# The packed token list of a mixture-of-experts stage gathered in two column parts, 352 and 224, with the first pair's products between them

## What is computed

```python
g_w, g_idx = lax.top_k(softmax(x @ w_router_group + b), 1)        # 1 of 4 groups
e_val, e_idx = lax.top_k(logits of the 8 experts in that group, 2)
combine = one_hot(expert_id, 32) * softmax(e_val) * g_w           # per token
gate = jnp.einsum("nd,edf->nef", x, p["w_gate"][l])
up = jnp.einsum("nd,edf->nef", x, p["w_up"][l])
hid = jax.nn.silu(gate) * up * combine
out = jnp.einsum("nef,efd->nd", hid, p["w_down"][l])
```

## Time and profile before

| what | us |
|---|---|
| median of 3 runs | 2022.97 (2018.91 to 2027.98) |
| the profiled execution | 2020.29 |
| its span, first to last instruction | 2017.7 |
| TensorE matmuls busy | 1750.8 (87%) |
| VectorE / ScalarE / GpSimd busy | 531.8 / 252.1 / 44.9 |
| mean granted TensorE clock | 0.94 |

### The profile page before, as it was taken

The page is one execution under the profiler, slowest core; times in us unless marked ns, Lnnn a source line. Parts: engine busy times, 40 slices in busy tenths (PEclk is TensorE's granted clock), DMA queues, the critical chain, the costliest instruction groups (busy, mean ns, idle before and its releaser), DMA issues.

```text
span 2017.7 us, 21998 instructions
## 1 busy us (share of the span) xinstructions
PE 1750.8 (87%) x8222; PEld 983.2 (49%) x8222; DVE 531.8 (26%) x1225; ACT 252.1 (12%) x456; POOL 44.9 (2%) x95
## 2 busy tenths in 40 slices
PE   3899999965999689999779999996879968899995
PEld 1477745321776234444337776442347743344442
DVE  1211200243212503334413021013521133233334
ACT  1110001110200221111021000101110021111111
POOL 0000000010000000000000000000100000000000
PEclk9999999987999689999989999998989987999998
DMA  9333334489633229999943233337883330898991
GB/s 400 130 118 135 126 125 146 157 358 370 262 125 118 91 112 381 393 407 394 367 191 147 100 150 126 125 126 319 342 351 117 139 149 7 344 377 364 380 371 68
DMA packets 32246, 454.38 MB, mean 225 GB/s; under 512 B 3632, under 2 KB 3632, under 8 KB 4752
## 3 DMA queue, kind: packets, MB, share of 16 engines
q1 hardware_dynamic: 27648, 402.67, 50.7%
q10 hardware_dynamic: 2304, 33.56, 4.1%
q0 software_dynamic: 2192, 16.75, 2.1%
HBM read 413.77 MB, written 39.19 MB: 224 GB/s over the span
## 4 chain that ended last, share of the span: by engine, by line
issue 38%; PE 37%; DMA 20%; DVE 2%; POOL 1%; ACT 0%; DVEq 0%; POOLq 0%; SPq 0%; ACTq 0%
PE ps L513 37%; DMA ring<-stream 16%; DMA state_sample_out<-ring 3%; DMA gfs<-gfin 1%; ACT work L863 0%; POOL rstd L430 0%; DVEq L1030 0%; POOL prm L452 0%; SPq L407 0%; POOLq L429 0%; DVE work L1066 0%; DVE xT L1450 0%; DVE ring L1381 0%; DVE stats L1037 0%; DVE hT L1464 0%
## 5 line engine op out<-in xcount | busy, mean ns | idle before, releaser
L513 PE MATMUL ps<-ring,work 128*64 128x512 f32 x1536 | 357.7, 616 | 47.5 <-DMA ring<-stream 38.4
L513 PE MATMUL ps<-ring,hT 128*32 128x128 f32 (+1 forms) x1920 | 320.6, 383 | 18.9 <-ACT hT L863 18.9
L513 PE MATMUL ps<-hT,ring 128*128 128x288 f32 x1280 | 316.0, 410 | 1.7 <-DVE work L1308 1.7
L513 PEld LDWEIGHTS ps<-hT,ring 128*128 128x128 f32 x1280 | 244.8, 192 | 70.9 <-DVE work L1308 1.9
L863 ACT ACTIVATE work<-ps 128x512 f32<-128x512 f32 (+4 forms) x256 | 118.8, 471 | 1171.3 <-PE ps L513 1170.7
L513 PE MATMUL ps<-work,ring 128*128 128x288 f32 x1024 | 249.6, 406 | 5.3 <-DVE work L1402 3.1
L513 PEld LDWEIGHTS ps<-ring,work 128*64 128x64 f32 x1536 | 118.2, 141 | 269.7 <-issue 251.0
L513 PEld LDWEIGHTS ps<-ring,hT 128*32 128x32 f32 (+1 forms) x1920 | 155.4, 137 | 185.2 <-issue 183.4
L513 PE MATMUL ps<-work 128*128 128x288 f32 (+6 forms) x800 | 225.7, 426 | 14.0 <-DVE work L1066 12.1
L513 PEld LDWEIGHTS ps<-work,ring 128*128 128x128 f32 x1024 | 194.2, 190 | 59.9 <-issue 6.6
L513 PEld LDWEIGHTS ps<-work 128*128 128x128 f32 (+2 forms) x800 | 136.4, 197 | 103.8 <-issue 80.5
(11 more groups left out here) (180 smaller groups left out, 763.2 us busy)
## 6 DMA issues: line engine op xcount, KB each, us to landing
ring<-stream SPq DMA_DIRECT2D x192, 2048.0 KB, 9.8
state_sample_out<-ring ACTq DMA_DIRECT2D x16, 2048.0 KB, 8.8
prm<-params POOLq DMA_DIRECT2D x3, 2640.5 KB, 9.5
state_out<-prm POOLq DMA_DIRECT2D x8, 512.0 KB, 8.9
cst<-consts POOLq DMA_DIRECT2D x1, 1649.5 KB, 13.9
xT<-x_in POOLq DMA_DIRECT2D x1, 1152.0 KB, 20.9
y_out<-hT POOLq DMA_DIRECT2D x1, 1152.0 KB, 4.4
v_out<-work POOLq DMA_DIRECT2D x2, 128.0 KB, 5.0
```

The source lines that it names most:

```text
L513: ins = nc.tensor.matmul(out, lhsT, rhs, start=start, stop=stop, **k)
```

## The change

The 576 places are cut in `HEAD` = 352 = 288 + 64 and `TAIL` = 224 columns. The windows of the first pair cannot reach beyond 352: expert 0 begins at 0 and expert 1 at 288 at most, each 64 wide.

- VectorE builds `psel` for the first 352 columns, raises `sel_ready`, and then builds the other 224 and raises it again.
- TensorE gathers 352 columns into each of g0 to g7, then makes the broadcasts and pair 0's gate/up products. Behind these it gathers the 224 columns, two k in a tile, in four new tiles g0 to g3 of pair 0 (banks 5, 6, 7, 5), and goes on with pair 0's transposes. The tile g8 is gone, and the three broadcast tiles move on by a bank.
- ScalarE copies pair 0's windows right behind the head tiles, ahead of the broadcasts, and into a buffer of its own (`first_xs`, over `yslot`), since `psel` is still needed. Behind the SiLU of pair 0 it evicts the four new tiles, then copies the windows of pairs 1 and 2.
- GpSimd waits with the parameter load for the last of the new tiles.

```diff
@@ -27,6 +27,8 @@
 CAP = 64
 OCAP = 128
 PACK = 2 * TOK
+HEAD = TOK + CAP
+TAIL = PACK - HEAD
 HGW = PACK + OCAP
 PAIRS = NE // 2
 NOVER = (2 * TOK) // (CAP + 1)
@@ -81,7 +83,7 @@
     if kind == "ysum":
         return []
     if kind == "route":
-        return ["lg", "lgt"] + [f"h{j}" for j in range(6)] + ["rk", "cnt", "ob"] + [f"g{k}" for k in range(KT + 1)] + ["bc0", "bc1", "bc2"]
+        return ["lg", "lgt"] + [f"h{j}" for j in range(6)] + ["rk", "cnt", "ob"] + [f"g{k}" for k in range(KT)] + ["bc0", "bc1", "bc2"]
     return ["t"]
 
 
@@ -93,7 +95,8 @@
 TILES["ysample"] = (YBANK, used[YBANK])
 used[YBANK] += 1
 for p in range(PAIRS):
-    for name, b in [("gu", p % 2), ("t", 2), ("y0", 3), ("y1", 4)] + [(f"c{ft}", 5 + (KT * p + ft) % 3) for ft in range(KT)]:
+    late = [(f"g{k}", 5 + k % 3) for k in range(KT // 2)] if p == 0 else []
+    for name, b in late + [("gu", p % 2), ("t", 2), ("y0", 3), ("y1", 4)] + [(f"c{ft}", 5 + (KT * p + ft) % 3) for ft in range(KT)]:
         TILES[("pair", p), name] = (b, used[b])
         used[b] += 1
 LAYER_USES = list(used)
@@ -296,6 +299,7 @@
         part = X(TOK)
         diag = cut(ovd[:, 0:3 * 4 * P], 3 * 4, P)
         xs.append(W(place[0], KT, P))
+        first_xs = cut(yslot, KT, P)
         rt, prod, ein, e2, oh8, oh8b = X(3, 36), X(3, NE), X(3, 8), X(3, 8), X(3, 8), X(3, 8)
         g4, g4b, eg, col = X(3, 4), X(3, 4), X(3, 4), X(16, 3)
         oh1, oh2, cnt, slots, picked = X(3, NE), X(3, NE), X(3, NE), X(3, NE), X(3, NE)
@@ -391,6 +395,10 @@
 
         def taken(ins, name):
             ins.then_inc(acc_free[bank(name)], 1)
+
+        def xs_of(p):
+
+            return first_xs if p == 0 else xs[p % 2]
 
         def row(ap, index):
 
@@ -472,7 +480,7 @@
 
                 pool.wait_ge(rf_stored, l * (16 * HEADS) + 16 * HEADS)
                 wait_made(pool, (("route", 0), "bc2"), l)
-                wait_made(pool, (("route", 0), f"g{KT}"), l)
+                wait_made(pool, (("pair", 0), f"g{KT // 2 - 1}"), l)
                 pool.wait_ge(tables_ready, l + 1)
                 pool.dma_start(prm[:, :], row(params, l + 1)).then_inc(params_loaded, 16)
                 for p in range(PAIRS):
@@ -764,15 +772,10 @@
                         mm(out[:, NE:2 * NE], nbb[0:NE, :], C("tri")[0:NE, 0:NE], True, True)
                         made(mm(out[:, 2 * NE:3 * NE], nbb[0:NE, :], C("tri_incl")[0:NE, 0:NE], True, True), (step, "ob"))
 
-                        pe.wait_ge(sel_ready, l + 1)
+                        pe.wait_ge(sel_ready, l * 2 + 1)
                         for k in range(KT):
                             out = wait_free(pe, (step, f"g{k}"), l, [(step, f"h{j}") for j in range(6)] if k == 0 else ())
-                            made(gather(out[:, :], k, slice(0, 512)), (step, f"g{k}"))
-                        out = wait_free(pe, (step, f"g{KT}"), l)
-                        rest = PACK - 512
-                        for k in range(KT):
-                            last = gather(out[:, k * rest:k * rest + rest], k, slice(512, PACK))
-                        made(last, (step, f"g{KT}"))
+                            made(gather(out[:, 0:HEAD], k, slice(0, HEAD)), (step, f"g{k}"))
 
                         pe.wait_ge(counts_ready, l * 3 + 3)
                         for tt, rows in TTILES:
@@ -785,9 +788,16 @@
                     w = [cut(pair_slot(3 * p + q, l)[:, :], KT, 512) for q in range(2)]
                     for k in range(KT):
                         for q in range(2):
-                            last = mm(out[64 * q:64 * q + 64, :], xs[p % 2][:, k, CAP * q:CAP * q + CAP], w[q][:, k, :],
+                            last = mm(out[64 * q:64 * q + 64, :], xs_of(p)[:, k, CAP * q:CAP * q + CAP], w[q][:, k, :],
                                       k == 0, k == KT - 1, skip_group_check=True)
                     made(last, (("pair", p), "gu"))
+                    if p == 0:
+                        pe.wait_ge(sel_ready, l * 2 + 2)
+                        for n in range(KT // 2):
+                            out = wait_free(pe, (("pair", 0), f"g{n}"), l)
+                            for k in (2 * n, 2 * n + 1):
+                                last = gather(out[:, k % 2 * TAIL:k % 2 * TAIL + TAIL], k, slice(HEAD, PACK))
+                            made(last, (("pair", 0), f"g{n}"))
 
                     if p >= 1:
                         for half in range(2):
@@ -866,6 +876,22 @@
                 wait_read(act, (("st", b), f"1{HEADS - 1}"), l)
                 r = SLOT_OF["st", b] % RING
                 act.dma_start(row(state_sample_out, l * NB + b), ring[r][:, :]).then_inc(slot_free[r], 16)
+
+            def silu_gate(out, dst, experts):
+                gate = cut(out, experts, 2, 64)[:, :, 0, :]
+                return apply(dst, gate, ACT.Silu)
+
+            def windows(p, l):
+
+                at = [act.value_load(offi[0:1, 2 * p + q:2 * p + q + 1], min_val=0, max_val=PACK) for q in range(2)]
+                if p == 0:
+                    wait_reads(act, [(("route", 0), f"g{k}") for k in range(KT)], l)
+                if p == 1:
+                    wait_reads(act, [(("pair", 0), f"g{k}") for k in range(KT // 2)], l)
+                    act.wait_ge(tables_ready, l + 1)
+                for q in range(2):
+                    last = apply(xs_of(p)[:, :, CAP * q:CAP * q + CAP], hg[:, :, bass.ds(at[q], CAP)], ACT.Copy)
+                last.then_inc(xs_ready, 1)
 
             act.wait_ge(consts_loaded, 64)
 
@@ -966,37 +992,25 @@
                                 apply(col[:, 8, :], col[:, 7, :], ACT.Exp).then_inc(exp_out, 1)
                         for k in range(KT):
                             out = wait_made(act, (step, f"g{k}"), l)
-                            taken(apply(hg[:, k, 0:512], out[:, :], ACT.Copy), (step, f"g{k}"))
-                        out = wait_made(act, (step, f"g{KT}"), l)
-                        taken(apply(hg[:, :, 512:PACK], cut(out[:, :], KT, PACK - 512), ACT.Copy), (step, f"g{KT}"))
-                        act.wait_ge(offsets_ready, l + 1)
+                            if k == KT - 1:
+                                act.wait_ge(offsets_ready, l + 1)
+                            taken(apply(hg[:, k, 0:HEAD], out[:, 0:HEAD], ACT.Copy), (step, f"g{k}"))
+                        windows(0, l)
                         for tt, rows in TTILES:
                             out = wait_made(act, (step, f"bc{tt}"), l)
                             taken(apply(rows4[:, :, tt * P:tt * P + rows], cut(out[:, 0:4 * rows], 4, rows), ACT.Copy), (step, f"bc{tt}"))
                 assert n_var == VARS
 
-                def silu_gate(out, dst, experts):
-                    gate = cut(out, experts, 2, 64)[:, :, 0, :]
-                    return apply(dst, gate, ACT.Silu)
-
-                def windows(p):
-
-                    at = [act.value_load(offi[0:1, 2 * p + q:2 * p + q + 1], min_val=0, max_val=PACK) for q in range(2)]
-                    if p == 0:
-                        wait_reads(act, [(("route", 0), f"g{k}") for k in range(KT + 1)], l)
-                    if p == 1:
-                        act.wait_ge(tables_ready, l + 1)
-                    for q in range(2):
-                        last = apply(xs[p % 2][:, :, CAP * q:CAP * q + CAP], hg[:, :, bass.ds(at[q], CAP)], ACT.Copy)
-                    last.then_inc(xs_ready, 1)
-
-                windows(0)
-                windows(1)
                 for p in range(PAIRS):
                     out = wait_made(act, (("pair", p), "gu"), l)
                     silu_gate(out[:, :], hid[:, :, :], 4).then_inc(silu_ready, 1)
+                    if p == 0:
+                        for n in range(KT // 2):
+                            out2 = wait_made(act, (("pair", 0), f"g{n}"), l)
+                            taken(apply(hg[:, 2 * n:2 * n + 2, HEAD:PACK], cut(out2[:, 0:2 * TAIL], 2, TAIL), ACT.Copy), (("pair", 0), f"g{n}"))
+                        windows(1, l)
                     if p + 2 < PAIRS:
-                        windows(p + 2)
+                        windows(p + 2, l)
                     out = wait_made(act, (("pair", p), "t"), l)
                     taken(apply(hidT[:, :], out[:, 0:2 * P], ACT.Copy), (("pair", p), "t"))
                     out = wait_made(act, (("pair", p), "y0"), l)
@@ -1058,13 +1072,14 @@
 
             def build_sel():
 
-                for tt, rows in TTILES:
-                    dve.tensor_scalar(psel[0:rows, tt, :], C("iota")[0:rows, :], packed[0:rows, tt, 0:1], None, ALU.is_equal)
-                settle()
-                for tt, rows in TTILES:
-                    sel = psel[0:rows, tt, :]
-                    last = dve.scalar_tensor_tensor(sel, C("iota")[0:rows, :], packed[0:rows, tt, 1:2], sel, ALU.is_equal, ALU.add)
-                last.then_inc(sel_ready, 1)
+                for cols in (slice(0, HEAD), slice(HEAD, PACK)):
+                    for tt, rows in TTILES:
```

(6 more changed lines are left out.)

## The result

| kernel | median us | ratio to before, 95% interval |
|---|---|---|
| before | 2025.7 | 1 |
| changed | 2040.8 | 1.0069 (1.0046 to 1.0092) |

The change makes the kernel slower by 0.7%, about 14 us (0.0069 x 2026), where I had forecast 5 us faster. The profiled execution of the changed kernel has a span of 2040.0 us.

What follows compares the result with a forecast made beforehand. The expert weight stream and, before it, the wait for GpSimd's free of pair 0's slots bound the kernel. 8.8 earlier minus 6.4 for the load gives 2.4 us per layer, 4.8 in all: 2022.97 to 2018, range 2006 to 2030.

Steps and rivals of the forecast that it cites:

- 1, earlier first product: VectorE's selection matrix for the last 224 columns no longer stands before the first product: gain 1.05 us, bounds 0.9 and 1.4.
- restart earlier by: Ring restart after the gather: 739.3 against 748.09 in layer 0, 1715.4 against 1724.2 in layer 1, 8.8 us earlier each.
- Step 2: TensorE's eight head tiles of 352 columns, with the earlier low-clock stretches kept: 24.9 us in layer 0, 21.8 in layer 1.
- Rival (b): The 224-column tail loses the full clock, taking 24.0 us instead of 13.0: 17 us slower in all, 2040; chance 0.13.
- Steps 4 and 5: TensorE's 224-column tail takes 13.0 us at full clock; tail's end to ring restart 1.6 us, restart 8.8 earlier per layer.
- step 3: From last head tile to pair 0's products 3.55 us through ScalarE's windows, broadcasts in that gap; products then 7.1 us.
- Step 6: Parameter load beside the ring's restart shares the DMA engines: costs 6.4 us per layer, bounds zero and 6.9.
- rival (a): Idle DMA time absorbs the parameter load: whole 8.8 us per layer gained, 17.6 in all, 2005; chance 0.27.
- the swap of the two: TensorE's wait moves from pair 2 to pair 1: 1.7 us counted on pair 1 cancels against pair 2.
- Rival (c): Pair 0's slots come free as soon as its products end: 23 us per layer earlier, 33 in all, 1990; chance 0.

Runs made afterwards that it cites:

- e4: Changed kernel with the gather cut at 512 and 64 columns instead of 352 and 224: ratio to before 0.9998.
- e5: Changed kernel with three unread 512-column products put ahead of the gather, in TensorE's idle time: ratio to before 0.9911.
- e6: Changed kernel with the parameter load issued early, in the stream's hole, slots still held behind the second gather part: ratio to before 1.0003.
- e3: Kernel before with the early parameter load alone: ratio to before 1.0003.
- e7: Kernel before with three unread 512-column products put ahead of its gather: ratio to before 0.9944.
- e2: Changed kernel with pair 0's two gate/up slots given back as its products end, the parameter load issued after the second gather part: ratio to before 1.0009.
- e1: Changed kernel with the parameter load issued early and pair 0's slots no longer held for the second gather part: ratio to before 1.0027.
- e9: e1 with ScalarE's eviction of pair 0's transposes ahead of the copies for pairs 1 and 2: ratio to before 0.9957.
- e8: e9 plus three unread 512-column products ahead of the gather: median 1985.6 us, ratio to before 0.980.

## Why the prediction was wrong, point by point

| step | forecast, layers 0 and 1 | measured |
|---|---|---|
| 1, earlier first product | 1.05 us | 1.06 |
| 2, first part | 24.9, 21.8 | 33.0, 33.0 |
| 3, last head product to pair 0 | 3.55, with pair 0 in 7.1 | 3.8 and 4.4, pair 0 in 7.09 and 7.23 |
| 4, second part | 13.0 | 12.3 |
| 5, tail's end to restart | 1.6 | 1.0 |
| restart earlier by | 8.8, 8.8 | 1.9, -2.1 |
| 6, price of the load | 6.4 | 5.4, 5.6 |

**Step 2 failed.** I read from the earlier trace rows that the clock was low for 15.1 and 8.5 us and carried these times over to another sequence of products ("I keep both"). The runs showed no rise at all: 0.50 for the whole 33.0 us, in both layers. Even for 512 columns the time to the rise was no constant, from 4.6 to 15.1 us in before and e4. For 352 columns no row existed. The honest bounds were "at once", 17.8 us by my full-clock price (8 x 2.22), and "never", 33.7 us by my half-clock price (8 x 4.21; measured 33.0). The upper one would have moved the forecast by 8.8 + 11.9 us to 16 us slower, against 14 measured. The prices of a product were good: 2.22 us a tile at full clock (2.16 measured in e5), 1.63 in the tail (1.53). Over both layers step 2 came out 19.3 us too short in the forecast, and all other steps together 3 us too long. Either fault of the changed kernel can be mended alone: without the load beside the ring it is as fast as before (e6), without the low clock 0.9% faster (e5). The forecast had counted the load and not the clock.

**Rival (b) had the right mechanism in the wrong place.** It looked for the lost clock in the 224 columns and gave it 0.13. They had the full clock in every run that has them, 12.3 us each time. The place to look was the first part, which begins at half clock. e5 shows what that start is worth at one and the same column count: 17.3 us from 1.00, 33.0 from 0.50.

**Steps 4 and 5 were right, and step 3 up to the clock.** I had ScalarE's windows as the limit of step 3 and the broadcasts, at full clock, under them. At half clock the broadcasts took 3.94 and 4.50 us and became the limit themselves. Where the clock was full the step came out as forecast, 3.54 us in e5, with TensorE waiting for ScalarE:

```profile
707.57 2.40 PE L521 MATMUL ps<-ovd,ones 128*128 128x512 f32 x6
711.11 7.09 PE L521 MATMUL ps<-ring,work 128*64 128x512 f32 x32 [1.14 <-ACT work L876]
```

The order of GpSimd was read rightly: the ring restarted 0.24 us behind the load's issue, in layer 1 0.25. The reason given for the size of the gain, that pair 0's slots stay behind the whole gather, is what the profile shows. One reading at the start was loose: the DMA line of the earlier trace rows has its only zero in layer 1; for layer 0 the hole shows in the earlier trace rows, as a DMA share of 0.00.

**Step 6 was right in kind and near in size.** 5.4 and 5.6 us against 6.4, so at most 1 us was absorbed and rival (a), which needed less than 3.7, fell. e4 and e5 had the same wait: 12.9 to 13.6 us from restart to pair 1 in their four layers. By the rule of the Trainium skill ("DMA: Bandwidth & Descriptors", "Issuing engines are not separate DMA queues"), transfers of different issuing engines interleave on the same 16 DMA engines; the traces agree, with 12.9 to 13.6 us beside the load (changed, e4, e5) and 7.5 to 8.1 without (before, e3, e7). Pair 1's products ran 8.78 us, as counted, and pair 2's 7.1 in both layers, so the swap of the two was right too.

**Rival (c) was excluded rightly and priced wrongly.** I gave it 23 us per layer for slots free at once. e2 did just that and gained some 12 us over the changed kernel in all, no more than e6, which only moved the load (13 us). The price left out that four slots are all there are, and that the third is held by products behind the second part.

**What sets pair 1's start, seen from the runs:** three limits stand close behind one another there. Counted from the ring's restart in layer 0, the slot with the load beside it comes after 13.1 us (changed); TensorE's own queue, with its 3.9 us of waiting for ScalarE's row of copies, is through after 8.4 us there and 9.2 in e6; and the slot without the load comes after about 7.7 (before). The forecast knew the first and called the second covered, which held only while the first was late.

## What to carry to other kernels

When an edit changes the shape or the density of products behind an idle stretch of TensorE, price them at both clocks and let the range reach to "the clock never comes back"; don't carry over the duration of the low stretch. Products put into the idle time just ahead can be a cheap remedy: here three of them, in some 5 us of idle time per layer, bought 31 us in the changed kernel and 11 in before. And when work is moved ahead of a queue's restart, look at what else used the quiet time, here a 2.7 MB load that was free in before (e3) and held pair 1 up by 5.5 us per layer after.

## What the runs showed of the hardware

- First parts of 352 columns without added products ran all 33.0 us at 0.50 in each layer of five kernels (changed, e1, e2, e6, e9), ten of ten. First parts of 512 columns got the full clock after 15.1 and 8.5 us in before, 14.9 and 9.0 in e3, and 4.6 and 8.9 in e4, six of six. So 48 instructions of 512 columns took less time (26.0 and 28.1 us in e4) than 48 of 352.
- The 64-column products, at full clock when they began, lost it in all eight gathers that had them, while TensorE was busy throughout: after 4.5 to 5.7 us in before, e3 and e4, and after 1.7 and 1.8 us in e7. 224-column ones kept it for 12.3 us, 352-column ones for 17.3 (e5, e8).
- Which property of the sequence decides was not tried: the columns, the row heights of 128 and 32, or the short gaps between instructions. Nor was it tried whether filling the idle time with other products than those of 512 columns would do.
- Adding some 5 us of products per layer that nobody reads made two different kernels faster, by 0.6% and 1.6%.
